# Gated delta rule in a hybrid block: gates of two blocks spread at once, exponents on ScalarE, lower matrices held as 64x64 blocks, keys and values turned behind the inversion

## The reference, cut to what matters

```python
decay = jnp.exp(jnp.where(incl, gc[..., :, None] - gc[..., None, :], -jnp.inf))
lower = jnp.where(strict, jnp.einsum('bhncd,bhnsd->bhncs', k_beta, k) * decay, 0.0)
t_inv = lax.linalg.triangular_solve(eye + lower, jnp.broadcast_to(eye, lower.shape),
                                    left_side=True, lower=True, unit_diagonal=True)
u = jnp.einsum('bhncs,bhnsd->bhncd', t_inv, v_beta)
w = jnp.einsum('bhncs,bhnsd->bhncd', t_inv, k_beta * jnp.exp(gc)[..., None])
...
v_new = u_c - jnp.einsum('bhcd,bhde->bhce', w_c, state)
o = jnp.einsum('bhcd,bhde->bhce', q_c, state) + jnp.einsum('bhcs,bhse->bhce', a_c, v_new)
state = state * jnp.exp(gl)[..., None, None] + jnp.einsum('bhcd,bhce->bhde', k_c, v_new)
```

## Time and profile before

| | |
|---|---|
| runs (3) | 2381.65 us median, 2379.84 to 2381.73 |
| the profiled execution | 2382.03 us, its span 2380.2 us |
| TensorE busy | 2340.7 us, 98% of the span, 11798 products |
| VectorE, ScalarE, GpSimd busy | 890.0, 771.4, 1283.1 us |
| granted TensorE clock, mean | 0.996 of full speed |

### The profile page before, as it was taken

How to read it: one execution, slowest core, us unless ns; L and a number is a source line. 1 busy time by engine, 2 the same in 40 slices (tenths; PEclk the granted TensorE clock), 3 DMA queues, 4 the chain that set the end, 5 groups by cost and what they waited for, 6 DMA issues and landing times.

```text
span 2380.2 us, 29590 instructions
## 1 busy us (share of the span) xinstructions
PE 2340.7 (98%) x11798; PEld 1917.6 (81%) x11798; DVE 890.0 (37%) x1404; ACT 771.4 (32%) x1537; POOL 1283.1 (54%) x732
## 2 busy tenths in 40 slices
PE   8999999999999999999999999999999999999998
PEld 7798877787877888888887988767778778888887
DVE  3653314343355431123356523243443445211233
ACT  5533325323136231122355442262140353211121
POOL 5511653564553566677655126635555535666774
PEclk9999999999999999999999999999999999999999
DMA  4300331332231333333223013313322313333331
GB/s 152 98 27 28 89 89 53 98 89 72 79 100 44 106 107 97 98 98 98 80 77 89 19 36 91 87 47 113 89 80 71 93 49 95 119 98 97 97 95 66
DMA packets 105753, 196.84 MB, mean 83 GB/s; under 512 B 8464, under 2 KB 18832, under 8 KB 105360
## 3 DMA queue, kind: packets, MB, share of 16 engines
q1 hardware_dynamic: 104464, 188.65, 26.2%
q10 hardware_dynamic: 1152, 6.29, 0.8%
HBM read 192.82 MB, written 2.10 MB: 82 GB/s over the span
## 4 chain that ended last, share of the span: by engine, by line
PE 91%; DVE 5%; ACT 3%; issue 1%; DMA 0%; DVEq 0%; ACTq 0%
PE big L1686 66%; PE mix L1686 9%; PE mix L1824 5%; DVE c_lo L1429 1%; PE big L2000 1%; PE mix L1968 1%; PE mix L1894 1%; PE mix L2069 1%; PE mix L1979 1%; PE mix L1787 1%; PE mix L2201 1%; PE mix L2150 0%; DVE scr L1441 0%; PE mix L1741 0%; PE mix L2134 0%
## 5 line engine op out<-in xcount | busy, mean ns | idle before, releaser
L568 POOL TENSOR_SCALAR ring_hi<-stage 128x1024 fp32r<-128x1024 f32 (+3 forms) x364 | 372.1, 1022 | 1042.6 <-PE big L1686 962.2
L570 POOL TENSOR_TENSOR ring_lo<-stage,ring_hi 128x1024 fp32r<-128x1024 f32 (+3 forms) x364 | 912.6, 2507 | 30.4
L1686 PE MATMUL big<-h_hi,ring_hi 128*128 128x512 f32 (+1 forms) x1888 | 720.3, 382 | 2.8 <-DVE h_lo L1149 1.5
L1686 PE MATMUL big<-h_hi,ring_lo 128*128 128x512 f32 (+1 forms) x1888 | 709.9, 376 | 0.0
L1686 PE MATMUL big<-h_lo,ring_hi 128*128 128x512 f32 (+1 forms) x1888 | 709.9, 376 | 0.0
L1686 PEld LDWEIGHTS big<-h_hi,ring_hi 128*128 128x128 f32 x1888 | 355.7, 188 | 75.3 <-issue 9.0
L1686 PEld LDWEIGHTS big<-h_lo,ring_hi 128*128 128x128 f32 x1888 | 355.6, 188 | 65.4
L1686 PEld LDWEIGHTS big<-h_hi,ring_lo 128*128 128x128 f32 x1888 | 355.8, 188 | 63.8 <-issue 1.9
L1628 DVE TENSOR_TENSOR h_lo<-scr,h_hi 128x1024 fp32r<-128x1024 f32 x64 | 84.7, 1324 | 248.4 <-ACT h_hi L1067 248.4
L1686 PE MATMUL big<-ring_hi,h_hi 128*128 128x512 f32 x448 | 174.5, 391 | 0.0
L1686 PE MATMUL big<-ring_lo,h_hi 128*128 128x512 f32 x448 | 174.3, 391 | 0.0
(11 more groups left out here) (292 smaller groups left out, 2826.3 us busy)
## 6 DMA issues: line engine op xcount, KB each, us to landing
stage<-in_w_in SPq DMA_DIRECT2D x168, 512.0 KB, 3.5
stage<-in_w_mlp_in SPq DMA_DIRECT2D x64, 512.0 KB, 3.6
stage<-in_w_mlp_out SPq DMA_DIRECT2D x64, 512.0 KB, 3.8
stage<-in_w_o SPq DMA_DIRECT2D x16, 512.0 KB, 3.8
stage<-in_w_br_a SPq DMA_DIRECT2D x8, 512.0 KB, 3.8
stage<-in_w_br_c SPq DMA_DIRECT2D x8, 512.0 KB, 3.8
stage<-in_w_br_d SPq DMA_DIRECT2D x8, 512.0 KB, 3.9
stage<-in_w_br_b SPq DMA_DIRECT2D x8, 512.0 KB, 3.5
```

Source lines behind the costliest of these rows:

```text
L568: nc.gpsimd.tensor_scalar(rH[jw][0:pp, r, 0:kk, 0:job.n], w, 1.0, 0.0, ALU.mult, ALU.add).then_inc(sem("w_hi"), 1)
L570: nc.gpsimd.tensor_tensor(rL[jw][0:pp, r, 0:kk, 0:job.n], w, f32(rH[jw][0:pp, r, 0:kk, 0:job.n]), ALU.subtract).then_inc(sem("w_ready"), 1)
L1686: ins_ = MM(o_, a_, r_, start=s0, stop=s1)
```

## The change

- **Spread.** A product "gt" turns the small columns of gates and beta of all blocks into 16 rows for either two of the four heads; VectorE rounds them to fp32r and puts the rest in 16 further rows (`g_rows`). R and B of a block are then two fp32r products of 256 columns each, whose weights are one selecting column (`CROW`, new constants). R and B of blocks 0 and 1 are made together, behind the first half of "av"'s third unit and its second half.
- **Exponents.** `row_exponents` on ScalarE makes relu(gc - R) for each head, exp of R, and exp of the negated relu: for the 64x64 diagonal blocks (`g_decc`), the last column (`s_ed`) and all. VectorE keeps `beta_keys`.
- **Compact lower matrices.** LT holds for each head the two diagonal 64x64 blocks, one in rows 0 to 63 and one in rows 64 to 127 of the same 64 columns, and the block between them apart. Masks, LTm, T and V have 256 columns for four heads and not 512.
- **Inverse.** Levels 1 to 5 are made for the two halves, with products of 64 rows by 64 columns, at array rows and columns 0 to 63 and 64 to 127 by turns. Y, X and V (but for V of level 5) have 32 columns for a head. One tile now holds four heads, so there are two tiles (e) in turn, not four. T0 and V are products with the identity, not transposes. Level 6 is one 64x64 product chain, from the lower left block, written into U.
- **Order.** kn and vn of the first block of a pair stand behind the levels. Of the three fills ahead of the levels two are made as two halves of two units; the single units in the recurrence of blocks 0 to 2 are cut in halves, one ahead of LT and new and one behind them.
- **Edges.** The gate copy of tile 0 of the last quarter in stick breaking stands ahead of two exponentials; the store of the last token tile is made in two halves, each behind its own half of the sum.

```diff
@@ -276,22 +278,19 @@
...
-    k += ["gc", ("R", 0), ("B", 0)] + [("raw", i) for i in range(8, 12)]
-    k += [("LT", 0), ("att", 0), ("R", 1), ("B", 1), ("LT", 1), ("att", 1)]
+    k += ["gc", "gt", ("R", 0), ("B", 0), ("R", 1), ("B", 1), ("LT", 0), ("att", 0), ("LT", 1), ("att", 1)]
+    k += [("raw", i) for i in range(8, 12)]
     for b0 in (0, 2):
-        k += [("T0", b0), ("T0", b0 + 1), ("kn", b0), ("vn", b0)]
+        k += [("T0", b0), ("T0", b0 + 1)]
...
-                k += [(t, b0 + e, n, c) for e in range(2) for c in range(2)]
+                k += [(t, b0 + e, n) for e in range(2)]
         for b in (b0, b0 + 1):
             ahead = b + 2 < NT
-            if b > b0:
-                k += [("kn", b), ("vn", b)] + ([("att", b + 1)] if ahead else [])
+            k += [("kn", b), ("vn", b)] + ([("att", b + 1)] if ahead and b > b0 else [])
             k.append(("ks", b))
-            k += [("R", b + 2), ("B", b + 2)] if ahead else []
-            k.append(("new", b))
-            k += [("LT", b + 2)] if ahead else []
-            k += [("o", b), ("dS", b)]
+            k += [("R", b + 2), ("B", b + 2), ("LT", b + 2)] if ahead else []
+            k += [("new", b), ("o", b), ("dS", b)]
         if b0 == 0:
             k.append(("att", 3))
...
@@ -399,12 +401,19 @@
...
+        g_dec, g_U = [by_head(1), by_head(3)], [by_head(2), by_head(4)]
+
+        HALVES = (slice(0, HB), slice(HB, P))
+        blocks = lambda ap: ap.rearrange("p (h c) -> p h c", c=HB)
+        g_T, g_LT, g_LTm = ([scr[:, gslot(i):gslot(i) + GH * HB] for i in two_] for two_ in ((1, 3), (10, 11), (14, 15)))
+        g_V = [g_uc[:, GH * HB * e:GH * HB * (e + 1)] for e in range(2)]
...
+        eR_of = lambda b: g_kd if b == 1 else g_eR
+        g_LTq = [scr[0:HB, gslot(i) + GH * HB:gslot(i) + 2 * GH * HB] for i in (10, 11)]
+        g_Yc = [scr[:, gslot(i):gslot(i) + GH * HB // 2] for i in (16, 17)]
+        g_Yq = [scr[HB:P, gslot(i):gslot(i) + GH * HB] for i in (16, 17)]
...
@@ -752,57 +758,67 @@
...
+            def row_exponents(b):
+
+                e, R = b % 2, heads(mix_wait(act, ("R", b)))
+                if b > 1:
+                    act.wait_ge(*upto("a_attd", b - 1))
+                mix_freed(act, "gc")
+                for h in range(GH):
+                    A(g_dec[e][:, h, :], R[:, h, :], ACT.Relu, bias=s_gc[:, b, h:h + 1], scale=-1.0).then_inc(sem("a_arg"), 1)
...
+                mix_free(A(eR_of(b), R, ACT.Exp), ("R", b))
+                act.wait_ge(*upto("a_arg", 4 * b + 4))
+                for rows in HALVES:
+                    A(blocks(g_decc[e])[rows], g_dec[e][rows, :, rows], ACT.Exp, scale=-1.0).then_inc(sem("a_decc"), 1)
+                A(s_ed[:, b, :], g_dec[e][:, :, P - 1], ACT.Exp, scale=-1.0).then_inc(sem("a_ed"), 1)
+                act.wait_ge(*upto("a_ed", b + 1))
+                act.wait_ge(*upto("a_decc", 2 * b + 2))
+                A(g_dec[e], g_dec[e], ACT.Exp, scale=-1.0).then_inc(sem("a_dec"), 1)
...
+            row_exponents(0)
+            row_exponents(1)
+            lower_copy(0)
+            conv_raw(8)
+            conv_raw(9)
+            lower_copy(1)
+            conv_raw(10)
+            conv_raw(11)
...
+                        ps = mix_wait(act, ("Y", b0 + e, n))
+                        if n < LEVELS - 1:
+                            i = A(g_Yc[e], ps[:, 0:GH * HB // 2], ACT.Copy)
+                        else:
+                            i = A(g_Yq[e], ps[HB:P, 0:GH * HB], ACT.Copy)
+                        mix_free(i, ("Y", b0 + e, n))
+                    for e in range(2) if n < LEVELS - 1 else ():
+                        ps = mix_wait(act, ("V", b0 + e, n))
+                        if n < LEVELS - 2:
+                            i = A(level_half(g_V[e], n, 1), ps[:, 0:GH * HB // 2].rearrange("p (m z) -> p m z", z=1 << n), ACT.Copy)
+                        else:
+                            for rows in HALVES:
+                                i = A(g_U[e][rows, :, rows], blocks(ps[rows, 0:GH * HB]), ACT.Copy)
+                        mix_free(i, ("V", b0 + e, n))
...
+                        row_exponents(b + 2)
+                        lower_copy(b + 2)
...
@@ -899,10 +915,12 @@
...
+                if p == 3:
+                    gate_c_copy(p, (0,))
                 for e in range(2):
                     act.wait_ge(*upto("c_sum", place(sum_order, p, 3 + e)))
                     stick_weights(p, e)
-                gate_c_copy(p)
+                gate_c_copy(p, (1,) if p == 3 else range(2))
...
@@ -1293,16 +1316,19 @@
...
+                rows, cols = slice(32 * e, 32 * e + 16), slice(e * P, (e + 1) * P)
+                TS(g_rows[rows, cols], ps[rows, cols], 1.0, None, ALU.mult).then_inc(sem("a_rhi"), 1)
+            for e in range(2):
+                rows, low, cols = slice(32 * e, 32 * e + 16), slice(64 + 32 * e, 80 + 32 * e), slice(e * P, (e + 1) * P)
+                dve.wait_ge(*upto("a_rhi", e + 1))
+                i = TT(g_rows[low, cols], ps[rows, cols], f32(g_rows[rows, cols]), ALU.subtract)
+            mix_free(i, "gt")
...
@@ -1311,35 +1337,41 @@
...
+                dve.wait_ge(*upto("a_decc", 2 * b + 2))
+                TT(ps, ps, blocks(g_decc[e]), ALU.mult).then_inc(sem("a_lt"), 1)
...
+                TT(blocks(g_LTq[e]), blocks(bank[0:HB, GH * HB:2 * GH * HB]), g_dec[e][0:HB, :, HB:P], ALU.mult).then_inc(sem("a_ltq"), 1)
...
-                mix_free(TT(g_Uall[e], pairs(per_mask(ident)), pairs(ps), ALU.subtract), ("LT", b))
+                dve.wait_ge(*upto("a_one", 2))
+                one = ident_c.unsqueeze(1).to_broadcast((P, GH, HB))
+                mix_free(TT(blocks(g_V[e]), one, ps, ALU.subtract), ("LT", b))
...
@@ -1348,44 +1380,44 @@
...
+            for b in range(2):
+                beta_keys(b)
+            for b in range(2):
+                lower(b)
+                scores_out(b)
+                first_level(b)
...
+            row_decays(0)
...
+                    if n < LEVELS - 2:
                         for e in range(2):
                             level_mask(b0 + e, n + 1)
...
+                        key = ("X", b0 + e, n)
+                        ps = mix_wait(dve, key)
+                        if n < LEVELS - 1:
+                            t = level_half(g_T[e], n, 0)
+                            i = TT(t, t, ps[:, 0:GH * HB // 2].rearrange("p (m z) -> p m z", z=1 << n), ALU.subtract)
+                        else:
+                            i = TS(g_U[e][0:HB, :, HB:P], blocks(ps[0:HB, 0:GH * HB]), -1.0, None, ALU.mult)
+                        mix_free(i, key)
+                    if n == 1:
+                        row_decays(b0 + 1)
...
+                    natural_k_v(b)
+                    if b == 1:
+                        scores_out(2)
+                        row_decays(2)
...
@@ -1804,11 +1839,14 @@
...
-                if i == 2:
                     pe.wait_ge(*upto("a_g", 2))
                     ps = tile_of("gc")
                     done(MM(ps[:, 0:16], triu, s_g.rearrange("p b h -> p (b h)"), start=True, stop=True), "gc")
-                    decays(0)
+                if i == 2:
+                    mix_freed(pe, "gc")
+                    ps = tile_of("gt")
+                    MM1(ps[0:16, 0:P], s_begc[:, 0, :], ident)
+                    done(MM1(ps[32:48, P:2 * P], s_begc[:, 1, :], ident), "gt")
...
+                mix_freed(pe, "gt")
+                for name, row in (("R", 8), ("B", 0)):
+                    ps = tile_of((name, b))
+                    for q in range(2):
+                        at = CROW - CRD + row + 2 * b + q
+                        i = MM1(ps[:, 2 * P * q:2 * P * (q + 1)], rot_r[:, at:at + 1].to_broadcast((P, P)), g_rows[:, :])
+                    done(i, (name, b))
...
+                ps, near = tile_of(("LT", b)), slice(0, HB)
+                for h in range(GH):
+                    k, kb = tokens(aK, h, b), g_kb[b % 2][:, h, :]
+                    for rows in HALVES:
+                        MM1(ps[rows, h * HB:(h + 1) * HB], k[:, rows], kb[:, rows])
+                    i = MM1(ps[near, (GH + h) * HB:(GH + h + 1) * HB], k[:, near], kb[:, HB:P])
+                done(i, ("LT", b))
...
@@ -1841,80 +1890,104 @@
...
+            for i in range(2):
+                unit(JOB["av"], i)
+                value_unit(i)
+            unit(JOB["av"], 2, (0, 1))
+            value_unit(2)
+            unit(JOB["av"], 2, (2, 3))
+            decays(0)
+            decays(1)
+            unit(JOB["av"], 3, (0, 1))
...
+            lower(0)
+            scores_gdn(0)
+            unit(JOB["av"], 3, (2, 3))
+            lower(1)
+            scores_gdn(1)
+            set_fill("gatea0", "az")
+            for tiles in ((0, 1), (2, 3)):
+                for q in range(2):
+                    unit(*fills[q], tiles)
+            del fills[0:2]
             fill(1)
...
+                    ps = tile_of(("T0", b0 + e))
+                    for h in range(GH):
```

(58 more changed lines are left out.)

233 lines of the change are left out of this document (67 added, 166 removed), and 10 rows, old and new, of the table PER_LAYER.

## The result

The changed kernel takes 2356.86 us (median of 4 runs, 2354.03 to 2363.43), the kernel before on the same chip 2380.97; the ratio is 0.9903, 95% interval 0.9891 to 0.9916. So it is 24 us faster. I had forecast 2333.0, a gain twice as large; the time lies inside my range, near its upper end, next to the 2358 of rival (c) and 7 us above the 2350 of rival (b), mild. The profiled execution was the slowest of the four: 2363.43 us, span 2361.6.

A forecast was written before the change was run, and what follows sets the result against it. TensorE's own queue was taken as the bound, a level by its number of records. Terms -36 (levels), -8.6 (spread), -2 (keys and values), -1.5 and -0.7 (edges) sum to -48.8: 2382.0 to 2333 us; own range 2323 to 2346, wider to 2358.

The forecast's parts named there:

- rival (c): Stretch between the pairs: 5 to 8 us of new VectorE and ScalarE waits replace 1.3; 2358 us, chance 0.06.
- rival (b): Inversion levels: the granted clock falls there; 2350 us or, at worst, 2389 us; chance 0.22 in all.
- mild: Levels' clock falls, but only moving data and ends slow: +0.4 a level, 1.5 after the stage; 2350 us, chance 0.14.
- The levels' term: Four inversion stages with levels 1 to 5 on 64x64 blocks: 18.5 us each against 27.5, -36 us.
- the full clock: Levels: continuous records keep full clock, so 2333 us stands; forecast's chance 0.65.
- the hard case: Levels' clock falls and weight loads slow too: a pair of records 0.11 us, a stage 30.0; 2389 us, chance 0.08.
- Block 3's: Recurrence, block 3: TensorE reaches LT 1.3 us before VectorE is ready.
- The term -8.6: Spread of gates: R and B as fp32r products save 10.5 us, gt and its wait cost 1.9.
- Lower matrices: Three 64-column products a head for one of 128: taken as 0, from -0.2 to +0.4 each, 8 times.
- Keys and values: kn and vn turned behind the levels, covering their waits for VectorE: -2 us, from -6 to +4.
- edges: Gate copy of tile 0 in stick-breaking moved ahead, -1.5 us; last store halved, -0.7 us.
- half of the gate copies' term: Stick-breaking's gate copy ahead of two exponentials removes TensorE waits: -1.5 us in all, from -2.5 to 0.

The follow-up runs named there:

- e3: Changed kernel with the moving data of Y, X and V sent twice in levels 1 to 5 (V: 1 to 4), 64 columns for 32: 2350.26 us.
- e6: Changed kernel with e1 and e3, row decays of block 2 behind block 3's beta keys, and ScalarE copying new before block 3's lower matrices: 2339.94 us.
- e9: e6 without the second copy of the moving data in the levels, so 32 columns again: 2354.38 us.
- e1: Changed kernel with three empty places added to the list of mixer tiles, making its PSUM bank rotation a multiple of four again: 2355.34 us.
- e11: e6 with VectorE instead of ScalarE copying V of the second block into U in the last level: 2334.97 us.
- e10: e6 with the gates spread as in the kernel before, 8 fp32 products a block for R and B: 2346.45 us.
- e8: Kernel before with the new spread of the gates alone, banks kept at a multiple of four: 2382.8 us.

## Why the prediction was half right

**The step that failed is the one that let the levels keep full clock.** The levels' term was -36 us; in the profiled execution it is 92.6 - 110.0 = -17.4. I had the risk as rival (b) with 0.22 in all, and the row that speaks for it, and still gave the full clock 0.65. It was the rule here, not the exception: the clock fell in three of four stages of the profiled execution. e3, and the pair of e6 and e9, show that it is the second copy of the moving data that keeps the clock up; TensorE's busy time doesn't tell the cases apart. Against the full clock the four stages lost 10.6 us (92.6 and 82.1 in e6), and what follows them or follows a wait some 6 more (LT and att of block 3 took 3.62 us in layer 0 where blocks 0 and 1 took 2.23; kn to the end of the spread of block 2 took 4.5 in layer 1 and 2.5 in e3; the transposes at the boundary 1.97 for 1.24 in e1; and their counterparts in the other layer). I had cited the Trainium skill, "TensorE: Matmul & The Clock Gate", for the rule that the clock is let go after idleness; the third stage, busy for 26.25 of 26.61 us at 0.65, disagrees with it, and the measurement decides.

**The time lies near rivals (c) and (b), mild, but by the mechanism of neither alone.** I had said that in the mild case the loads keep their pace. They don't: in the third stage pairs of records start 0.107 us apart (1303.091, 1303.198, 1303.304), which is the price of the hard case (0.11). It is reached for a part of the levels only, and that part changes from run to run. Rival (c), new waits in the recurrence, came true for the two stretches with block 3 (3.3 us of wait in each), not for 24 us. That the sum of all this falls inside my range, which was drawn for other causes, is luck.

**The size of a level at full clock was nearly right.** A pair of records takes 0.058 us for 0.055, a period 3.13 for 3.0. In the second stage, at full clock, it took 2.3 us until the first X, as said, 12.8 for the four periods where I had 12.0, and 5.2 from X of level 5 to the end where I had 4.2. The end was mis-sized because ScalarE's four copies of V and two of Y stand in one line; e11 takes part of it back. A stage is 20.5 us (82.1/4), not 18.5: 8 us of the shortfall.

**Waits behind VectorE.** Block 3's was named, at 1.3 us a layer; it was 3.3, because I priced VectorE's products by their usual 0.68 us where GpSimd's product can hold one for 2.84. The trace of the kernel before had shown it (2.88 at 118.31). 4 us.

**The layer boundary.** Missing from the sum. 4.1 us of wait. I read the list of tiles for its order and not for its length.

**Spread.** R and B of two blocks took 0.95 us (first record 92.85, the next unit 93.80), as said (0.96). The term -8.6 was -6.5 (e10). But I booked it as standing on TensorE's records alone; e8 gained nothing from them. In e8 the exponents' passes are 1.1 us of a wait of 3.84, and the product held beside GpSimd's is more, so which part of the new surroundings (the exponents on ScalarE, the new order of VectorE's work, the later readers) lets the spread count is not shown.

**Lower matrices.** LT and att of a block took 1.99 us from the first record to the next unit (96.65, 98.64), before 1.72 (114.36, 116.08): +0.27 for my 0, inside my bounds, some 2 us in all.

**Keys and values, edges.** The waits for kn, vn and the gate copy are gone as said. The single edges weren't tried.

The profiled executions can be compared without remainder, by the limits of the stages (us; in the forecast column kn and vn leave the stages with 1.3 us each and stand behind them, and half of the gate copies' term goes to each layer):

| stretch | before | after | change | forecast |
|---|---|---|---|---|
| to the first T0 | 121.6 | 120.1 | -1.5 | -1.7 |
| the four stages, kn and vn inside before | 116.3 | 92.6 | -23.7 | -41.2 |
| between the two stages of a layer, twice | 59.2 | 67.6 | +8.4 | -2.6 |
| from layer 0's second stage to layer 1's first | 1092.6 | 1094.7 | +2.1 | -1.1 |
| behind the last stage | 990.4 | 986.6 | -3.8 | -0.2 |
| the -2 of keys and values, placed nowhere | | | | -2.0 |
| span | 2380.2 | 2361.6 | -18.6 | -48.8 |

So 30.2 us were missing. 17.5 lie in the stages: 18.6 in the levels (10.6 clock, 8.1 size), less 1.1 because kn and vn with their waits had taken 6.3 us of them and not 5.2. 11.0 lie between the stages of a layer: the wait for block 3's beta keys (6.6), the half clock behind the levels and behind that wait (some 5) and LT and att (1.1), against waits of 1.4 for vn that went and small differences. 3.2 lie at the boundary, its wait of 4.1 and 0.7 of half clock against small gains. The last stretch did 3.6 better than forecast; a wait of 0.7 ahead of new, which only the kernel before has, is part of it, and the rest I did not trace. With the causes mended the same design runs in 2339.9 us (e6) and, with one copy moved, in 2335.0 (e11).

## What to carry to other kernels

Cutting products into quarters of the array makes records cheap only while the clock stays; look in the trace for the granted clock of the thinnest products it has, and price the levels at both clocks. If the clock falls with narrow moving data, sending them twice can cost nothing: here 14 us at the median, and 18 between two profiled executions, came back for a broadcast. When a change alters how many tiles a loop takes from a rotation of banks, count them modulo the banks, and look at the far end of the rotation, a layer away. Before a product of VectorE is priced by its usual duration, look for the longest of its kind in the trace and for what ran beside it. A saving on the bounding engine counts only where what stands behind it is early enough: the same spread was worth 6.5 us or less than nothing.
